# Attention, mixing and FFN in one block, with the attention's results halved head by head in its last steps

## The reference: what is computed

```
proj = rms_norm(x) @ w_in            -> q, k, v, index q/k/weights, conv parts, gates ga, gb
a = sparse_attend(q, k, v)           top 256 keys by index score, 8 heads, 2 key heads, head size 64
b = cb * causal_dwconv(cc * cx)
mixed = sigmoid(ga) * (a @ w_pa) + sigmoid(gb) * (b @ w_pb)
x = x + mixed @ w_o
ua, ub = split(rms_norm(x) @ ffn_up)
x = x + (silu(causal_dwconv(ua)) * ub) @ ffn_down
```

## Time and profile before

| what | us |
|---|---|
| median of three runs (lowest, highest) | 1983.06 (1978.84, 1988.6) |
| the profiled execution, its own time | 1978.17 |
| its span | 1976.0 |
| mean granted clock of TensorE, share of full speed | 0.956 |
| TensorE busy | 1796.2 (91%) |
| VectorE, ScalarE, GpSimd busy | 1061.4, 506.5, 682.1 |

### The profile page before, as it was taken

One profiled execution on the slowest core, in us unless ns is written; L12 is line 12 of the kernel. 1 busy time (PEld: TensorE's weight loads), 2 busy tenths in 40 slices (PEclk: granted clock), 3 DMA queues, 4 the chain that ended last, 5 costly groups with the idle time before them and its releaser, 6 DMA issues. The chain is left out here.

```text
span 1976.0 us, 28433 instructions
## 1 busy us (share of the span) xinstructions
PE 1796.2 (91%) x11467; PEld 1686.3 (85%) x11467; DVE 1061.4 (54%) x1777; ACT 506.5 (26%) x735; POOL 682.1 (35%) x409
## 2 busy tenths in 40 slices
PE   4858899899999659978759999999999999999997
PEld 3734899899999637665559999999999999999997
DVE  3373776889986966645335345433334344433335
ACT  3253011111111035654532232111111111111215
POOL 0417133221222056674436114334333332322430
PEclk6888999999999869999979999999999999999998
DMA  7105211222221032253537111111111111111102
GB/s 247 38 7 171 54 43 38 61 81 71 87 82 38 3 108 86 87 167 106 188 112 252 43 33 54 43 42 42 53 42 42 42 42 42 53 42 32 43 16 88
DMA packets 130264, 144.42 MB, mean 73 GB/s; under 512 B 15773, under 2 KB 110333, under 8 KB 129765
## 3 DMA queue, kind: packets, MB, share of 16 engines
q1 hardware_dynamic: 113288, 77.39, 13.6%
q0 software_dynamic: 11920, 46.35, 7.1%
q10 hardware_dynamic: 4978, 19.59, 2.7%
HBM read 123.74 MB, written 19.13 MB: 72 GB/s over the span
## 5 line engine op out<-in xcount | busy, mean ns | idle before, releaser
L226 PE MATMUL ps<-act_hi,w_hi 128*128 128x358 f32 (+1 forms) x1080 | 243.0, 334 | 13.2 <-POOL act_lo L458 7.8
L542 POOL TENSOR_TENSOR w_lo<-w_raw,w_hi 128x1024 fp32r<-128x1024 f32 (+1 forms) x57 | 140.4, 2467 | 298.6 <-ACT w_hi L537 298.6
L226 PE MATMUL ps<-act_lo,w_hi 128*128 128x358 f32 (+1 forms) x1080 | 238.2, 329 | 0.0
L226 PE MATMUL ps<-act_hi,w_lo 128*128 128x358 f32 (+1 forms) x1080 | 238.2, 329 | 0.0
L226 PE MATMUL ps<-x_gain_hi,w_hi 128*128 128x358 f32 x1056 | 231.4, 327 | 0.0
L226 PE MATMUL ps<-x_gain_hi,w_lo 128*128 128x358 f32 x1056 | 231.2, 327 | 0.0
L226 PE MATMUL ps<-x_gain_lo,w_hi 128*128 128x358 f32 x1056 | 230.6, 326 | 0.0
L1041 DVE TENSOR_SCALAR_CACHE_REDUCE count_junk<-scores,candidate 128x384 uint8<-128x384 f32 (+6 forms) x217 | 200.9, 990 | 0.0
L226 PEld LDWEIGHTS ps<-act_hi,w_hi 128*128 128x128 f32 (+1 forms) x1080 | 186.1, 190 | 15.0 <-issue 11.1
L2697 DVE TENSOR_TENSOR xt<-xt,ps 128x1074 f32<-128x1074 f32 x88 | 112.1, 1274 | 144.8 <-PE ps L226 144.8
L226 PEld LDWEIGHTS ps<-act_hi,w_lo 128*128 128x128 f32 (+1 forms) x1080 | 187.5, 189 | 1.0
(11 more groups left out here) (393 smaller groups left out, 3221.4 us busy)
## 6 DMA issues: line engine op xcount, KB each, us to landing
w_raw<-in_ffn_up SPq DMA_DIRECT2D x44, 512.0 KB, 3.8
w_raw<-in_w_in SPq DMA_DIRECT2D x32, 512.0 KB, 3.8
w_raw<-in_ffn_down SPq DMA_DIRECT2D x12, 512.0 KB, 3.4
w_odd_raw<-in_ffn_down SPq DMA_DIRECT2D x10, 512.0 KB, 3.4
x_save<-xt SPq DMA_DIRECT2D x1, 4296.0 KB, 13.0
mix_b<-row ACTq DMA_DIRECT2D x8, 537.0 KB, 3.3
sig_a<-row ACTq DMA_DIRECT2D x8, 537.0 KB, 3.0
sig_a_in<-sig_a ACTq DMA_DIRECT2D x8, 537.0 KB, 4.4
```

The source lines that it names most:

```text
L226: last = pe.matmul(core.acc(out_set)[0:rows, c, :], w(k), b(k)[:, c * CH:(c + 1) * CH], start=(k == 0 and n == 0), stop=(k == kblocks - 1 ...
L542: eng.tensor_tensor(self.core.wl[slot][:, 0:width], self.core.wr[slot][:, 0:width], self.core.wh[slot][:, 0:width].bitcast(F32), ALU.subtr ...
```

## The change

Attention and mixing are put into one block, and the last steps of the attention are laid out anew:

- `attention_to_output` opens one block and passes it to both stages. The barrier at L1705 is gone; the mixing's queues follow directly. In its place TensorE waits for six increments of a new semaphore `split_lo` (all low parts written), SyncE for the last of the samples' value products, ScalarE for those and for the samples' results.
- The sample items end two rounds earlier (`LAST_ITEM = STEPS - 4`, that is 29), so 98 items lie in rounds 2 to 28.
- In rounds 29 to 32 one head's high part is written at the end of ScalarE's round, and its low part at the end of VectorE's, for the columns from 256 on (818 columns), in rounds 30 to 32 behind a weight's high part. In round 33 columns 128 to 255 of all heads follow, and columns 0 to 127 after the loop as before.
- The low part of weight tile 0 moves from GpSimd to VectorE, between the last two low parts. Those of tiles 1 and 2 stay on GpSimd, which now waits for all of `split_lo` before them.

The diff without its changes of indentation:

```diff
-def attention_stage(nc, core, hd, ahead):
+def attention_stage(nc, core, hd, ahead, block):
...
-    padded, split_hi = sem("padded"), sem("split_hi")
+    padded, split_hi, split_lo = sem("padded"), sem("split_hi"), sem("split_lo")
...
-    FIRST_ITEM, LAST_ITEM = 2, 31
+    FIRST_ITEM, LAST_ITEM = 2, STEPS - 4
...
+    SPLIT = STEPS - 4
+    EARLY, NEXT = slice(128 * SHORT, TW), slice(128, 128 * SHORT)
...
-    with nc.Block() as block:
...
@@ scalar @@
-                if STEPS - 4 <= t < STEPS - 1:
-                    ahead.hi(act, t - (STEPS - 4))
-                if t in (STEPS - 1, STEPS):
-                    if t == STEPS - 1:
-                        act.wait_ge(normed, NT - 1)
+            if SPLIT <= t < SPLIT + G:
+                g = t - SPLIT
+                if g == 0:
+                    act.wait_ge(normed, NT - SHORT)
                     act.wait_ge(s_valued, 2 * (NGRP + 1))
                     act.wait_ge(s_result, 2)
                     act.wait_ge(padded, 1)
-                    for g in range(2 * (t - STEPS + 1), 2 * (t - STEPS + 1) + 2):
-                        act.activation(core.rh[:, g, 128:TW], raw[:, g, 128:TW], ACT.Copy).then_inc(split_hi, 1)
+                else:
+                    ahead.hi(act, g - 1)
+                act.activation(core.rh[:, g, EARLY], raw[:, g, EARLY], ACT.Copy).then_inc(split_hi, 1)
+            if t == STEPS:
+                act.wait_ge(normed, NT - 1)
+                act.activation(core.rh[:, :, NEXT], raw[:, :, NEXT], ACT.Copy).then_inc(split_hi, 1)
...
@@ gpsimd @@
-            ahead.lo(pool, 0)
             pool.wait_ge(valued, STEPS)
+        pool.wait_ge(split_lo, G + 2)
             for n in range(1, 3):
                 ahead.lo(pool, n)
...
@@ vector @@
-                if t in (STEPS - 1, STEPS):
-                    for g in range(2 * (t - STEPS + 1), 2 * (t - STEPS + 1) + 2):
+            if SPLIT <= t < SPLIT + G:
+                g = t - SPLIT
                 dve.wait_ge(split_hi, g + 1)
-                        dve.tensor_tensor(core.rl[:, g, 128:TW], raw[:, g, 128:TW], core.rh[:, g, 128:TW].bitcast(F32),
-                                          ALU.subtract)
-            norm(NT - 1, 2)
-            dve.wait_ge(split_hi, G + 1)
-            dve.tensor_tensor(core.rl[:, :, 0:128], raw[:, :, 0:128], core.rh[:, :, 0:128].bitcast(F32), ALU.subtract)
+                dve.tensor_tensor(core.rl[:, g, EARLY], raw[:, g, EARLY], core.rh[:, g, EARLY].bitcast(F32),
+                                  ALU.subtract).then_inc(split_lo, 1)
+            if t == STEPS:
+                dve.wait_ge(split_hi, G + 1)
+                dve.tensor_tensor(core.rl[:, :, NEXT], raw[:, :, NEXT], core.rh[:, :, NEXT].bitcast(F32),
+                                  ALU.subtract).then_inc(split_lo, 1)
+                ahead.lo(dve, 0)
+        norm(NT - 1, 2)
+        dve.wait_ge(split_hi, G + 2)
+        dve.tensor_tensor(core.rl[:, :, 0:128], raw[:, :, 0:128], core.rh[:, :, 0:128].bitcast(F32), ALU.subtract)\
+            .then_inc(split_lo, 1)
+    return Handover(split_lo, G + 2, s_valued, 2 * (NGRP + 1), s_result, 2)
...
-def mix_and_ffn_stage(nc, core, wm):
+def mix_and_ffn_stage(nc, core, wm, block, attention):
...
-    with nc.Block() as block:
...
@@ sync @@
+        sp.wait_ge(attention.s_valued, attention.sample_values)
             fetch_d(1, 1)
...
@@ tensor @@
+        pe.wait_ge(attention.split_lo, attention.splits)
             for t in range(2 * KB):
...
@@ scalar @@
+        act.wait_ge(attention.s_valued, attention.sample_values)
+        act.wait_ge(attention.s_result, attention.sample_results)
             gates(0)
             gates(1)
...
+def attention_to_output(nc, core, hd, ahead):
+    with nc.Block() as block:
+        attention = attention_stage(nc, core, hd, ahead, block)
+        mix_and_ffn_stage(nc, core, ahead.w, block, attention)
```

More of the change, by code:

```diff
@@ L1703, in diagonal @@
         return raw[p, :, a:a + 16].rearrange("p g (b t) -> p g b t", t=DS), src
-    with nc.Block() as block:
[L1707 to L1766, removed]
-                else:
[L1768 to L1780, removed]
@@ new lines, in _, with low, gather, gathers @@
+    @block.gpsimd
+    def _(pool):
+        def low(s, x):
+            pool.wait_ge(hi, count[s] + x + 1)
+            _, p_hi, p_lo, p_raw = piece(s, x)
+            pool.tensor_tensor(p_lo, p_raw, p_hi.bitcast(F32), ALU.subtract).then_inc(lo, 1)
+        def gather(m, b4):
+            sg, y = divmod(m, 8)
+            slot, grp = 4 * (m % 2) + b4, y % 4
+            a = (4 * sg + b4) * NGA + grp
+            pool.indirect_dma_start(
+                out=got[slot][:], out_offset=None, in_=keys if y < 4 else values_,
+                in_offset=bass.IndirectOffsetOnAxis(ap=core.rows[:, a:a + 1], axis=0),
+            ).then_inc(gathered[slot], 16)
+        def gathers(y):
+            sg, x = divmod(y, ITEMS)
+            r, what = divmod(x - 1, 3)
+            grp, half_of = divmod(x - VT0, 2)
+            if 0 < x < 25 and what == 1 and r % 2:
+                m = 8 * sg + r // 2 + 2
+                pool.wait_ge(keys_turned, 2 * (NGRP * sg + r) + 2)
@@ L2001, in _ @@
                 for b4 in range(4):
                     gather(m, b4)
-            pool.memset(raw[:, :, TOK:TW], 0.0).then_inc(padded, 1)
-            for t in range(STEPS + 2):
-                s = t - 1
-                for x in range(PARTS):
-                    if x == 0 and 0 <= s < STEPS:
-                        low(s, 0)
-                    if x >= 2 and 0 <= s < STEPS and x - 1 < len(pieces(s)):
-                        low(s, x - 1)
-                    for y in items(t, x):
-                        gathers(y)
@@ L2115, in mix_and_ffn_stage @@
-def mix_and_ffn_stage(nc, core, wm):
+            if VT0 <= x and half_of == 1 and grp < NGRP and grp % 2 and 8 * sg + grp // 2 + 6 < 16:
+                m = 8 * sg + 4 + grp // 2 + 2
+                pool.wait_ge(s_valued, (NGRP + 1) * sg + grp + 1)
+                for b4 in range(4):
+                    gather(m, b4)
+        for m in range(2):
+            for b4 in range(4):
+                gather(m, b4)
+        pool.memset(raw[:, :, TOK:TW], 0.0).then_inc(padded, 1)
+        for t in range(STEPS + 2):
+            s = t - 1
+            for x in range(PARTS):
+                if x == 0 and 0 <= s < STEPS:
+                    low(s, 0)
+                if x >= 2 and 0 <= s < STEPS and x - 1 < len(pieces(s)):
+                    low(s, x - 1)
+                for y in items(t, x):
+                    gathers(y)
```

1615 lines of the change are left out of this document (827 added, 788 removed).

## The result

The changed kernel is slower: a median of 2004.43 us (1994.21 to 2005.58, five runs) against 1982.91 (1978.84 to 1988.6), a ratio of 1.0094 with a 95% interval of 1.0071 to 1.0116, or about +19 us (1.0094 of 1982.9; the medians themselves are 21.5 us apart). Its profiled execution took 1994.21 us, with a span of 1992.4. The forecast was 1977.4, with 1987 as the upper end.

What follows compares the result with a forecast made beforehand. TensorE's queue standing still bounded the kernel, its largest hole 13.2 us before the first mixing product. -8.1 (tail) + 4.4 (moved items) - 2.0 (smaller hole) = -5.7 us, 1977.4 against the median 1983.06; range 1969 to 1987.

Steps and rivals of the forecast that it cites:

- The tail: From step 29's exponential to the first mixing product: 25.1 us counted against 33.2 before, 8.1 us less.
- The block's 5.0 us: End of the attention's block, 1011.8 to 1016.8 us: this 5.0 us goes; lower bound of the gain 0.
- the contention: Last low parts: GpSimd's waiting removes VectorE's slowing beside it, 3.275 us for 946 columns against 1.135 alone.
- the chain through VectorE's queue: Last steps: the next copy queues behind the low half and ScalarE waits; 5.1 us a step against 2.74 bare.
- Rival A: Last steps: low halves don't delay the next copy, three steps stay near 3.5 us; -10.7 us, 1972.4, chance 0.19.
- When step 29 comes: Start of step 29 after packing the items: +4.4 us for moved items, -2.0 for a smaller hole.
- The eight items' own time: Items of steps 29 and 30, moved ahead of step 29: 9.84 us less 5.5 bare makes it 4.4 later.
- The hole at the second exponentials: Step 25: TensorE's 3.0 us wait shrinks as the exponentials move to steps 23 and 24; -2.0 us.
- Rival D: Longer last steps eat the block's end and step 25's hole merely moves; -3 to 0 us, about 1981.5, chance 0.15.
- Rival B: Steps 24 to 28: packed items meet late gathers, one more wait per value group; +4.7 us, 1987.8, chance 0.15.
- the items fall at other places in every step: Steps with sample items: the reason given for a bound of -5 to +6 us on the packing.
- The clock: First mixing product: 5.1 us at clock 0.50 left as is; a rival had it stay up, -2.5 us, chance 0.09.

Runs made afterwards that it cites:

- e1: Changed kernel with only the block's end taken away, sample items and low parts as in the kernel before; 0.9973 of the kernel before, -5.3 us.
- e5: e1 with weight 0's low part on VectorE and GpSimd's other weights waiting for all low parts; 0.9959 of the kernel before, -8.1 us.
- e6: e5 with the results' four low parts behind the last copy and weight 0's on GpSimd in round 31; 0.9949 of the kernel before, -10.1 us.
- e2: Kernel before with sample items ending in round 28 instead of 30, nothing else changed; 1.0089 of the kernel before, +17.6 us.
- e3: Changed kernel with the fetch of the first three weight tiles held back until the last gathered values were used; 1.0041 of the kernel before, +8.1 us.
- e10: Kernel before with the weight fetch held back until just before the gathers for value groups 4 and 5; 1.0031 of the kernel before, +6.1 us.
- e4: Changed kernel with the first group's 49 items in their old places and the second's in rounds 18 to 28; 1.0056 of the kernel before, +11.1 us.
- e9: Kernel before with every sample item one place earlier, three instead of two in round 2, still ending in round 30; 1.0042 of the kernel before, +8.3 us.
- e7: Changed kernel with the edits of e3 and e4 together; 1.0015 of the kernel before, +3.0 us.

## Why the prediction was wrong

**The tail: right, and for its reason.** -8.3 us against -8.1. The block's 5.0 us and the contention each have an experiment (e1, e5), the chain through VectorE's queue has a part of one (1.8 of the 3.0 us of e6). Rival A's premise, that the halves hide, is refuted by the 1.41 us in which ScalarE stood idle in each step.

**The step that failed is "When step 29 comes"**, in which the move of the items was priced at +4.4 - 2.0 = +2.4 us with a bound of -5 to +6. Measured: step 29's logits 23.1 us later after the attention's start. It has these parts:

- *The eight items' own time, +4.4.* This took 5.5 us for two bare steps. In e2, where the last steps are otherwise as before, the exponentials of steps 29 and 31 are 6.4 us apart (9.8 before), so taking the items out saves 3.4 there. What they cost where they went was not measured alone.
- *The hole at the second exponentials, -2.0.* The wait itself fell from 3.0 to 1.1 us, but in step 24 there were two more holes of 1.6 and 1.7 us around it and 8.9 us of low clock, and the step took 12.1 us. Rival D had this as "the hole merely moves"; it grew.
- *The fetch, about 6 us in the profiles (6.3 in both e3 and e10) and 6 to 10 in the runs (6.1 in e10, 7.6 to 10.5 in e3).* The prediction listed every DMA that the tail moves and left out the one that stays: the weight fetch hangs on step 24, and what moved past it were the gathers. It asked whether the distance in items between a gather and its use changes; it doesn't, but the waits for gathered values went from 3.7 to 9.1 us, 8.0 of them for the last four gathers, which nothing waited for before. Rival B had the right place and nearly the right price (3.7 us and low clock for each wait), but put it down to TensorE overtaking the gathers. It also has the items wrong: by the table `due` steps 24 to 28 hold 21 instead of 19, and not seventeen. Its point of decision, one wait more than allowed, was passed by one longer wait and the next part.
- *The items' places and number in the first half, 5 to 8 us (4.6 to 7.5 in e4; e9's 8.3 has some of the fetch in it).* The prediction gave "the items fall at other places in every step" as a reason for a bound and did not work it out, though the table `due` gives each item's place without any run. With it the 0.6 us in each of rounds 3 to 7 could have been read from the order of the queue: two halves of one group of keys next to each other, with ScalarE's copy of 0.6 us between them. The larger losses are where GpSimd's four gathers come to stand ahead of a low part (12.6 us of such waits against 5.8), which the prediction named as a reason for its bound and gave no price.
- *The rest, about 7 us in steps 18 to 28*, is open (e7). The sizes are from single edits and profiles that differ by some us in their low clock, so they need not add up to 23.1 exactly.

**The clock.** Of the two ways in which the first product could start, the low one came: the granted clock was 0.50 for the first 3.3 us instead of 5.1, behind a gap of 3.2 us. But in steps 31 and 32 the clock had already been at 0.50, so the gap was not what dropped it. Where it wasn't looked for the clock did cost: step 27, with the hole of 8.0 us, had 8.8 of its 15.3 us at half clock, against 0.3 us in e3, which has no such hole and gained 7.6 to 10.5 us in the runs. The Trainium skill ("TensorE: Matmul & The Clock Gate", section "Why this matters for your kernels") says that long gaps between bursts of matmuls drop the clock; this step agrees with it.

**The chances.** Slower by over 0.5% had 0.07. Rival B needed two more waits to turn slower; that the same edit would open three kinds of wait at once, on three engines, was in none of the cases.

## What to carry to other kernels

Where side work is woven into a main loop by a table, shifting or packing it is a new order for every queue: print the table of both versions, and look for neighbours that were apart before (e9: one place cost 8 us with nothing added, a part of it by the fetch). Transfers that are released by different kinds of event drift against each other when one kind is moved; the one that the edit doesn't touch belongs in the list too. And before a tail is shortened by moving work out of it, look at what in it can be had alone: here one block, one writer of low parts at a time, and low parts behind the last copy gave -10 us (interval -6 to -14) with no item moved.

## What the runs showed of the hardware that was not expected

- A fetch of 1.5 MB in six transfers, issued among the last four of five indirect gathers, took their landing from 6.2 to 9.7 us in the median and from 6.4 to 12.7 at most; held back behind them (e3), it left the last four at 4.9 to 5.7.
- GpSimd and VectorE, both subtracting in SBUF, slowed each other: in the kernel before VectorE's 946 columns took up to 3.275 us against 1.135 alone; in the changed kernel, with GpSimd idle, 512 columns took 0.69 us against 1.46. GpSimd's three weight tiles took 8.77 us together, where one alone has a median of 2.40.
- Executions of one kernel lie up to 13 us apart, and those with a lower mean granted clock are the longer ones (the kernel before, measured together with e1: 1978 to 1983 us at 0.954 to 0.957, 1984 to 1990 at 0.948 to 0.952). One profile of each is thus good for a step's waits and not for the whole.
